# Three k tiles of the next projection's first output tile, multiplied ahead at each boundary, in a two-layer decoder trunk on one core

## What is computed

```python
for l in range(2):
    h = h + 0.5 * rmsnorm(swiglu(rmsnorm(h, g[FFN1_PRE]), w_in[l, 0], w_out[l, 0]), g[FFN1_POST])
    hn = rmsnorm(h, g[MIX_PRE])
    u_pool, q, k, v, gate_pool, gate_attn = split(hn @ w_in[l])
    y_pool = pool_mixer(u_pool)                 # causal means over 2, 4, 8, 16 tokens
    y_attn = swa_attention(q, k, v) @ w_attn_proj[l]
    merged = sigmoid(gate_pool) * y_pool + sigmoid(gate_attn) * y_attn
    h = h + rmsnorm(merged @ w_o[l], g[MIX_POST])
    h = h + 0.5 * rmsnorm(swiglu(rmsnorm(h, g[FFN2_PRE]), ...), g[FFN2_POST])
```

## Time and profile before

| | us |
|---|---|
| median of 3 runs (1190.07 to 1190.86) | 1190.37 |
| the profiled execution | 1191.37 |
| its span | 1189.3 |
| PE busy | 1179.4 (99%) |
| PEld busy | 1149.5 (97%) |
| DVE, ACT, POOL busy | 712.3, 541.1, 457.9 |

### The profile page before, as it was taken

One profiled execution on the slowest core, in us unless ns is written; L12 is line 12 of the kernel. 1 busy time (PEld: TensorE's weight loads), 2 busy tenths in 40 slices (PEclk: granted clock), 3 DMA queues, 4 the chain that ended last, 5 costly groups with the idle time before them and its releaser, 6 DMA issues.

```text
span 1189.3 us, 23831 instructions
## 1 busy us (share of the span) xinstructions
PE 1179.4 (99%) x9310; PEld 1149.5 (97%) x9310; DVE 712.3 (60%) x1050; ACT 541.1 (45%) x761; POOL 457.9 (39%) x521
## 2 busy tenths in 40 slices
PE   8999999999999999999999999999999999999997
PEld 7999999999999999999999999999999999999986
DVE  5755444868665865544477554447676658755542
ACT  6433334536553553333355333345466545544441
POOL 1855500207212476542128545112063124865600
PEclk9999999999999999999999999999999999999999
DMA  9754457373355355545636553573734653754540
GB/s 323 253 180 158 127 186 224 97 231 107 90 151 188 123 181 176 175 128 179 217 112 213 177 168 119 195 209 111 240 108 101 175 181 107 229 195 160 188 165 35
DMA packets 197997, 198.69 MB, mean 167 GB/s; under 512 B 4368, under 2 KB 190864, under 8 KB 197920
## 3 DMA queue, kind: packets, MB, share of 16 engines
q1 hardware_dynamic: 197600, 197.27, 52.4%
q10 hardware_dynamic: 320, 0.34, 0.1%
HBM read 196.54 MB, written 1.05 MB: 166 GB/s over the span
## 4 chain that ended last, share of the span: by engine, by line
PE 97%; DVE 2%; DMA 1%; SPq 0%; ACT 0%; issue 0%; DVEq 0%
PE bank L505 28%; PE bank L506 28%; PE bank L504 28%; PE bank L736 2%; PE bank L738 2%; PE bank L737 2%; PE bank L640 1%; PE bank L825 1%; PE bank L820 1%; PE bank L631 1%; PE bank L779 1%; PE bank L538 1%; DMA raw<-in_ffn_w_in 1%; PE bank L539 1%; PE bank L564 1%; PE bank L790 0%
## 5 line engine op out<-in xcount | busy, mean ns | idle before, releaser
L504 PE MATMUL bank<-x_hi,w_hi 128*128 128x272 f32 (+1 forms) x1988 | 572.1, 288 | 2.0 <-DVE w_lo L1607 1.4
L505 PE MATMUL bank<-x_lo,w_hi 128*128 128x272 f32 (+1 forms) x1988 | 570.5, 287 | 0.0
L506 PE MATMUL bank<-x_hi,w_lo 128*128 128x272 f32 (+1 forms) x1988 | 568.6, 286 | 0.0
L939 ACT ACTIVATE w_hi<-raw 128x2048 fp32r<-128x2048 f32 (+2 forms) x208 | 348.8, 1684 | 412.5 <-PE bank L506 398.3
L1240 DVE TENSOR_TENSOR w_lo<-raw,w_hi 128x2048 fp32r<-128x2048 f32 (+3 forms) x203 | 419.7, 2073 | 158.8 <-ACT w_hi L939 153.8
L504 PEld LDWEIGHTS bank<-x_hi,w_hi 128*128 128x128 f32 x1988 | 375.8, 189 | 4.0 <-DVE w_lo L1607 1.7
L505 PEld LDWEIGHTS bank<-x_lo,w_hi 128*128 128x128 f32 x1988 | 375.3, 189 | 0.3
L506 PEld LDWEIGHTS bank<-x_hi,w_lo 128*128 128x128 f32 x1988 | 373.7, 188 | 0.0
L1807 POOL TENSOR_TENSOR hid_hi<-silu,up_r 128x272 f32 x88 | 136.5, 1552 | 163.4 <-DVE up_r L1385 145.4
L505 PE MATMUL bank<-hid_lo,w_hi 128*128 128x272 f32 x528 | 152.3, 289 | 0.0
L506 PE MATMUL bank<-hid_hi,w_lo 128*128 128x272 f32 x528 | 151.9, 288 | 0.0
(11 more groups left out here) (205 smaller groups left out, 1276.4 us busy)
## 6 DMA issues: line engine op xcount, KB each, us to landing
raw<-in_ffn_w_in SPq DMA_DIRECT2D x86, 1024.0 KB, 5.1
raw<-in_w_in SPq DMA_DIRECT2D x24, 1024.0 KB, 5.7
raw<-in_ffn_w_out SPq DMA_DIRECT2D x24, 768.0 KB, 4.4
raw<-in_ffn_w_out SPq DMA_DIRECT2D x24, 640.0 KB, 4.0
raw<-in_ffn_w_out SPq DMA_DIRECT2D x10, 1024.0 KB, 5.0
raw<-in_w_in SPq DMA_DIRECT2D x16, 512.0 KB, 5.2
raw<-in_w_attn_proj SPq DMA_DIRECT2D x32, 256.0 KB, 4.6
raw<-in_w_o SPq DMA_DIRECT2D x8, 1024.0 KB, 5.7
```

Source lines behind the costliest of these rows:

```text
L504: pe.matmul(ps[:, t0:T], w[0], a_hi[:, t0:T], start=start, stop=False)
L505: pe.matmul(ps[:, t0:T], w[0], a_lo[:, t0:T], start=False, stop=False)
L506: return pe.matmul(ps[:, t0:T], w[1], a_hi[:, t0:T], start=False, stop=stop)
L939: last = act.activation(hi, w, ACT.Copy)
```

## The change

At each of the five boundaries, three k tiles (2, 3, 4 for n = 0 and 2; 1, 2, 3 for n = 1) of output tile 0 of the next projection are computed ahead and in two pieces. The new `h` of a tile is the old `h` plus a factor times `y` times the token's root; so the product with it is the product of old `h` (piece 0), plus the product of `y` with its gains (piece 1) times the root.

- PE: `keep_dense` and the bank opener go. Ahead of the spread it runs the 3 x 3 matmuls of piece 0, which go into the bank of output tile 0, behind it the 3 x 3 of piece 1, into a bank of their own. In `deep_three`, output tile 0 leaves out these three k tiles. The sum moves from ahead of tile 2 of k = 6 to ahead of tile 5, the spread from ahead of tile 2 of k = 7 to ahead of tile 4.
- ACT and DVE: 6 operands more each (`early_high`, `early_low`) before a boundary. They lie in idle slots of `x_hi` and `x_lo` (n = 0, 2) or of `o_hi` and `o_lo` (n = 1, once the attention projection has read them).
- ACT, in the pre-norm: it copies piece 1 out of its bank into `y` tile 0 behind `x_hi` tile 5, and makes the hi part of the next unit in four quarters, behind `x_hi` tiles 3, 4, 5 and 6, instead of behind the pre-norm.
- DVE: it multiplies piece 1 by the spread root (`scale_early`) behind `normed(7)`. It makes the lo part of the next unit ahead of var and no longer waits for POOL's power there. When it takes output tile 0, it adds piece 1 and then multiplies by `r` (`with_early`). At the start of a layer it makes the combined gains `g_out` with 3 small instructions.

```diff
+EARLY_K = ((2, 3, 4), (1, 2, 3), (2, 3, 4))
+EARLY_OLD, EARLY_OUT = 2, 5
...
+def early_before(n):
+    return n // 3 * 2 * sum(len(ks) for ks in EARLY_K) + 2 * sum(len(ks) for ks in EARLY_K[:n % 3])
...
-                        for c in range(6):
+                        for c in range(1 if k in EARLY_K[(q - 2) // 2 % 3] else 0, 6):
                             high(c, k, 0, T)
                     x_tile(x_at + k, l)
                     for c in range(6):
@@ -558,6 +578,8 @@
                             sum_part(q, l, 0)
                         if (k, c) == SPREAD_AT:
                             spread_rms(q, l)
+                        if c == 0 and k in EARLY_K[(q - 2) // 2 % 3]:
+                            continue
...
-            def keep_dense(n, by):
-
-                for _ in range(n):
-                    pe.matmul(warm[:, 0:SEQ], by[:, 0, META:META + P], by[:, 1, META:T], start=True, stop=True)
-
-            def open_banks(banks, by):
-
-                for b in banks[0:CUT_TILES]:
-                    pe.matmul(bank[b][:, 0:T], by[:, 0, META:META + P], zeros[:, 0:1].to_broadcast([P, T]), start=True, stop=False)
+            def early_products(n, l, u, which, b, t0):
+                ks = EARLY_K[n]
+                pe.wait_ge(early_lo, early_before(l * 3 + n) + (which + 1) * len(ks))
+                if which == 0:
+                    unit_split(u, l if n < 2 else l + 1)
+                    tile_free((T_FFN_OUT[0], T_WO, T_FFN_OUT[1])[n] + 6, l, 0)
+                for at, k in enumerate(ks):
+                    hi, lo = early_operand(n, which, at)
+                    last = products(bank[b], weights(u, k, 0), hi, lo, at == 0, which == 1 and at == len(ks) - 1, t0)
+                if which == 1:
+                    last.then_inc(early_done, 1)
...
-                    pe.transpose(bank[SPREAD_BANKS[q // 2]][:, first:first + n], rt[0:n, 0:1].to_broadcast([n, P]),
+                    pe.transpose(bank[SPREAD_BANK][:, 0:n], rt[0:n, 0:1].to_broadcast([n, P]),
...
-                keep_dense(WARM_RMS, hid_hi)
+                n, u, (b, b_out) = 2 * f, (U_K, U_FFN_IN[0])[f], EARLY_BANKS[2 * f]
+                early_products(n, l, u, 0, b, 0)
                 spread_rms(4 * f + 1, l)
-                keep_dense(WARM_X, hid_hi)
-                open_banks((KVQ_BANKS, FFN_BANKS)[f], hid_hi)
+                early_products(n, l, u, 1, b_out, 0)
...
+            def early_high(n, l, which, at, columns):
+                k = EARLY_K[n][at]
+                src = (h, y)[which]
+                act.activation(early_operand(n, which, at)[0], src[:, k, :], ACT.Copy, scale=columns[:, k:k + 1]
+                               ).then_inc(early_hi, 1)
+            def pre_norm(n, columns, h_before, u, u_layer):
+                parts = split_parts(u, len(NEXT_SPLIT_AT))
                 square(n, 0, h[:, 0, :], h_ready, h_before + 1)
                 for k in range(1, KD):
+                    if k == EARLY_OLD:
+                        act.wait_ge(early_done, n // 2)
                     x_high(columns, h_before, k)
+                    if k == EARLY_OUT:
+                        act.activation(y[:, 0, :], bank[EARLY_BANKS[n // 2 % 3 - 1][1]][:, 0:T], ACT.Copy).then_inc(early_taken, 1)
+                    if k in NEXT_SPLIT_AT:
+                        if k == NEXT_SPLIT_AT[0]:
+                            act.wait_ge(raw_landed[u % RING], landed_at(u, u_layer))
+                            act.wait_ge(unit_done, u_layer * UNITS + u + 1)
+                        w, hi, _ = parts[NEXT_SPLIT_AT.index(k)]
+                        last = act.activation(hi, w, ACT.Copy)
+                        if k == NEXT_SPLIT_AT[-1]:
+                            last.then_inc(hi_done, 1)
                     if k > 1:
                         square(n, k - 1, h[:, k - 1, :], h_ready, h_before + k)
                 square(n, KD - 1, h[:, KD - 1, :], h_ready, h_before + KD)
...
-                if l + f > 0:
-                    split_hi(u0 + 3, l)
...
+                act.wait_ge(layer_consts, l + 1)
+                n, g_x = 2 * f, (g_cur[:, 2 * KD:3 * KD], g_next)[f]
+                for at in range(len(EARLY_K[n])):
+                    early_high(n, l, 0, at, g_x)
+                for at in range(len(EARLY_K[n])):
+                    early_high(n, l, 1, at, g_out[:, n * KD:(n + 1) * KD])
...
+                act.wait_ge(unit_done, l * UNITS + U_WO + RING)
+                for at in range(len(EARLY_K[1])):
+                    early_high(1, l, 0, at, g_cur[:, 4 * KD:5 * KD])
...
+                    if m == EARLY_K[1][-1]:
+                        for at in range(len(EARLY_K[1])):
+                            early_high(1, l, 1, at, g_out[:, KD:2 * KD])
...
+                for n, by in enumerate((0.5, 1.0, 0.5)):
+                    g_y, g_x = (g_all[:, ds(l * (NORMS * KD) + (2 * n + i) * KD, KD)] for i in (1, 2))
+                    dve.scalar_tensor_tensor(out=g_out[:, n * KD:(n + 1) * KD], in0=g_y, scalar=by, in1=g_x,
+                                             op0=ALU.mult, op1=ALU.mult)
...
+            def early_low(n, l, which, at, columns):
+                k = EARLY_K[n][at]
+                src = (h, y)[which]
+                hi, lo = early_operand(n, which, at)
+                dve.wait_ge(early_hi, early_before(l * 3 + n) + which * len(EARLY_K[n]) + at + 1)
+                dve.scalar_tensor_tensor(out=lo, in0=src[:, k, :], scalar=columns[:, k:k + 1], in1=hi.bitcast(F32),
+                                         op0=ALU.mult, op1=ALU.subtract).then_inc(early_lo, 1)
+            def early_lows(n, l, which, columns):
+                for at in range(len(EARLY_K[n])):
+                    early_low(n, l, which, at, columns)
+            def with_early(n, l, b, out, scale):
+                dve.wait_ge(early_scaled, l * 3 + n + 1)
+                dve.tensor_tensor(y[:, 0, :], bank[b][:, 0:T], y[:, 0, :], ALU.add).then_inc(early_sum, 1)
+                dve.wait_ge(early_sum, l * 3 + n + 1)
+                return dve.tensor_tensor(out, y[:, 0, :], scale[:, :], ALU.mult)
...
+                def scale_early():
+                    t0 = blocks(2 * n + 1, l)[0][0]
+                    dve.wait_ge(early_taken, l * 3 + n + 1)
+                    dve.tensor_tensor(y[:, 0, t0:T], y[:, 0, t0:T], spread[:, t0:T], ALU.mult
+                                      ).then_inc(early_scaled, 1)
...
+                    if k + 1 == KD - 1:
+                        scale_early()
...
+                    if j == 0 and early is not None:
+                        n, early_l = early
+                        with_early(n, early_l, FFN_BANKS[0], gate_r[:, 0, :], r).then_inc(tile_read, 1)
+                        continue
...
+                    split_lo(u0 + 3, l)
                     mean_square(4 * f, l)
-                    dve.wait_ge(rt_ready, l * NORMS + 4 * f + 1)
-                    split_lo(u0 + 3, l)
                     take_rms(4 * f, l)
-                    take_gate(f, l, 0)
+                    take_gate(f, l, 0, early=(1, l) if f == 1 else (2, l - 1))
...
+                n = 2 * f
+                early_lows(n, l, 0, (g_cur[:, 2 * KD:3 * KD], g_next)[f])
+                early_lows(n, l, 1, g_out[:, n * KD:(n + 1) * KD])
...
+                split_lo(41, l)
                 mean_square(2, l)
-                dve.wait_ge(rt_ready, l * NORMS + 3)
-                split_lo(41, l)
                 take_rms(2, l)
-                take(U_K, F_KV, l, KVQ_BANKS[0:2], lambda j, ps: dve.tensor_tensor(kT[:, j, :], ps, r[:, :], ALU.mult))
+                take(U_K, F_KV, l, KVQ_BANKS[0:2], lambda j, ps: with_early(0, l, KVQ_BANKS[0], kT[:, 0, :], r) if j == 0
+                     else dve.tensor_tensor(kT[:, j, :], ps, r[:, :], ALU.mult))
...
+                early_lows(1, l, 0, g_cur[:, 4 * KD:5 * KD])
                 take_y(0)
                 take_y(1)
+                early_lows(1, l, 1, g_out[:, KD:2 * KD])
...
-WARM_RMS, WARM_X = 10, 7
 CUT_TILES = 1
-SPREAD_BANKS = (0, 2, 2)
+EARLY_BANKS, SPREAD_BANK = ((6, 0), (0, 2), (0, 2)), 1
 META_STEP = 6
 HIGH_FIRST = 2
-SUM_AT, SPREAD_AT = (6, 2), (7, 2)
+SUM_AT, SPREAD_AT = (6, 5), (7, 4)
+NEXT_SPLIT_AT = (3, 4, 5, 6)
 FFN_BANKS, KVQ_BANKS = (0, 1, 6, 3, 4, 5), (6, 1, 2, 3, 4, 5)
```

40 lines of the change are left out of this document (27 added, 13 removed).

## The result

The changed kernel takes **1194.25 us** (median of 7 executions, 1192.18 to 1196.17) against 1190.07 us for the kernel before on the same chip (7 executions, 1189.84 to 1190.91): ratio 1.0035, 95% interval 1.0025 to 1.0045. It is 4.2 us slower. The forecast was 1189.3 with a range up to 1192.0: wrong in its sign, and outside the range. The profiled execution took 1195.46 us, its span 1193.6.

What follows compares the result with a forecast made beforehand. PE bounds the kernel, busy 99% of the span. Savings by layer: n = 0, 1.06 and 0.9; n = 1, -0.1 and -1.5; n = 2, 0.8; 1.1 us less in all gives 1189.3 us, range 1186.2 to 1192.0.

Steps and rivals of the forecast that it cites:

- part 5: End of the pre-norm: stepping both queues has POOL's sixth sum asked for at 224.36, the seventh standing behind DVE's split.
- part 4: ACT in the pre-norm: quarters and piece 1's copy make it as busy as DVE; squares come 0.3 to 0.5 late.
- part 2: DVE's pace in k = 1 to 4: of 1.12 us, all stays for n = 0 and 2, 0.75 or 0.45 for n = 1.
- The clock: PE's clock after the mixer: a few tenths of idle time should not lower it; no chance set aside.
- Part 1: PE's stream: 9 matmuls per boundary leave deep_three, 1.12 us each, 5.6 over five; the spread starts no later.
- Part 3: Operands made ahead after the mixer: post_var 0.87 us late in layer 1, 0.05 in layer 0; nothing before n = 0 and 2.
- Part 5, n = 1: Pre-norm's sum: one split of 2.29 us holds up the seventh sum; PE waits 0.8 (layer 0) and 1.1 (layer 1).
- The reading in which both share the speed: DVE and POOL ports: both go on slowed, the seventh sum takes 1.5 to 2 us and costs nothing; 1187.4 us.
- n = 0: Pre-norm's sum: it slips between two half splits; PE waits 0.05 us in layer 0, 0.2 in layer 1.
- n = 2: Spread at the new layer: var stands behind columns and split, at 228.7; PE waits 0.3 to 0.4 us.
- Behind the projection: After the projection: DVE is earlier, its split done; with_early costs one instruction of 0.44 us and nobody waits.
- The rival "slower": End of k = 6: split always ahead of seventh sum, sixth behind last x_lo; 2.6 more, 1193.0 us; chance 0.11.

Runs made afterwards that it cites:

- E5: Changed kernel with scale_early moved behind update 7 and ACT's copy of piece 1 behind the square of tile 4: 1191.68 us, ratio 1.0008 to the kernel before.
- E8: The changed kernel itself, timed once more beside the other runs: 1194.36 us, ratio 1.0032 to the kernel before.
- E7: Changed kernel with the next unit's split behind the pre-norm, sum and spread at old places, scale_early and piece 1's copy moved later: 1188.87 us, ratio 0.9984.
- E3: Kernel before with only the order moves (ACT's quarters, lo part ahead of var, later sum and spread), no products ahead: 1190.92 us, ratio 0.9999.
- E2: Changed kernel with only DVE's lo part of the next unit put back behind var and POOL's power: 1192.65 us, ratio 1.0012.
- E4: Changed kernel with the next unit's split back behind the pre-norm on both ACT (one whole hi part) and DVE: 1192.25 us, ratio 1.0010.
- E10: Kernel before without its unread matmuls between the norm's sum and the spread and behind it (10 and 7 per boundary): 1197.63 us, ratio 1.0057.
- E11: E7 with the combined gains made in FFN 1's output stage and nothing made ahead at layer 1's mixer boundary: 1187.51 us, ratio 0.9974.
- E1: Changed kernel with unread matmuls put back where PE waits, ahead of late sums and spreads: 1193.61 us, ratio 1.0021 to the kernel before.
- E12: E11 with eight unread matmuls ahead of PE's wait for first_lo in the first projection: 1187.51 us, ratio 0.9976.

## Why the prediction was wrong

**The step that failed** is the stepping of the two queues in part 5: "the sixth sum is asked for at 224.36". On that clock it came at 225.34 less 0.34 for the later start, 225.00: 0.64 us late. I had counted `scale_early` as 0.36 to 0.44 us of DVE and the copy of piece 1 as a shift of ACT, but had not followed rightly what they push: update 7 into the fifth sum (0.86 instead of 0.44), x_hi 7 behind it, and the squares queued behind x_hi 7. E5 shows it by moving the two: the sixth sum comes 0.73 us earlier, and the time falls by 2.7 us (medians); in the table the five boundaries give 2.3 of it, with n = 1 of layer 0 held against E8, where the clock didn't fall either. The blame I gave to ACT's quarters in part 4 ("the squares come 0.3 to 0.5 late") is right in size (0.3, E5 against E7), was in the stepping already (224.36 is 16.08 us after the norm's first sum; E3 and E5, with the quarters, have 16.00 and 15.99), and cost nothing where the split is behind (E2 against E4).

**A second term was mis-sized: what the saved matmuls bring.** In E5 PE's waits are the forecast's almost to the tenth (0.69 and 1.10 at the sums of n = 1, 0.41 at n = 2, 0.74 for the late root, none at n = 0). Yet its five boundaries take together 0.1 us more than before, where the forecast had 1.15 less. So 1.25 us more were lost. By estimate 0.8 of it is the refilling of the pipeline behind these four waits, 0.2 each, which the forecast left out; the rest is that the 1.12 per boundary don't stay whole (part 2 below).

**The clock.** "The few tenths of idle time ... should not lower it ... No chance is set aside for it." It fell in both profiled executions of the changed kernel, at different waits, for 1.55 us in one. In E10 it fell at five boundaries of five, at 1.1 to 2.4 us each. The Trainium skill ("TensorE: Matmul & The Clock Gate", Part 1) has the idle array at half its clock. The trace agrees on the two levels, and it goes further: in E10 PE stood still for no more than 1.18 us at a time, with matmuls in between, and the clock fell. My ground for setting it aside, that the first slices show a full clock though PE is not always busy there, was no ground: the nines of the page can't show a fall of 3.4 us, and in E3 and E11 the clock did fall there; in the execution of before it happened not to. And the unread matmuls were worth 7.0 us to the kernel before (E10).

Point by point:

- *Part 1, 9 matmuls or 1.12 us per boundary*: they are gone (45 in all). The spread of layer 0, n = 0 starts 2.47 us after the norm's first sum, before 2.52: right.
- *Part 2, "all of the 1.12 stays" for n = 0 and 2*: 0.80 and 0.83 at best (E7). In E7's trace at n = 0 of layer 0 the first real product starts 4.09 us after the norm's first sum instead of 3.94, and PE stands at the pre-norm's sum just as the seventh sum ends (17.66 and 17.61 us after the norm's first sum; before, 18.61 and 17.59). Before, there was 1.0 us of room between the two, less than the 1.12 to be saved. The later place of the sum, which the forecast reckoned with, gives room back; what it would keep without other waits, no run shows.
- *Part 3, the late root after the mixer*: post_var 0.87 late forecast; it starts at 994.17, 3.18 after the earlier trace rows, of which 2.40 are the whole kernel's shift: 0.78. Right in size and place, though the working has it twice: a split that ends at 992.0 would make post_var 1.0 late, not 0.87. In layer 0 the spread comes 0.05 later, as said.
- *Part 5, n = 1*: waits of 0.8 and 1.1 forecast, 1.17 and 1.57 idle measured, 0.2 more each with the refilling. The rule that the ports are locked for a whole instruction held: at n = 1 the split, asked for 0.06 us after the sixth sum, first stands behind it (2.87 us instead of 2.29), and then the seventh sum stands behind the split: the pair takes 3.54 us instead of some 1.9. The Trainium skill says so in "SBUF — State Buffer", section "Who interferes with whom", and the trace agrees. The reading in which both share the speed (1187.4) is refuted: it gave the seventh sum 1.5 to 2 us, and it took 2.62.
- *n = 0*: 0.05 and 0.2 forecast, 0.48 and 0.64 idle measured, by the late sixth sum.
- *n = 2*: 0.3 to 0.4 at the spread, 0.89 measured: var stands behind columns and split, as said, and all of it was 0.65 later (var at 626.75, 229.35 on the clock of the first boundary, against 228.7).
- *Behind the projection*: "nobody waits there" was right for the changed kernel. But E4 shows what the split's place ahead of var was good for: without it, with PE 1.1 us earlier, each boundary waits 0.45 to 0.72 us idle for that split. I had named this cover nowhere.
- *The rival "slower"* came nearest, with a chance of 0.11. Its deciding point was 228.4 on that clock; at n = 1 of layer 0 the seventh sum ended at 420.09, which is 228.7. Its prices fit too (0.3 kept at n = 0 of layer 0, where the table has 0.32; 0 at n = 2, 0.01), and its 1193.0 lacks mainly the clock. But the way there was another, and so the fit is in part luck: the sixth sum did not wait behind the last x_lo (it took 0.77), it was asked for late, and at n = 2 the seventh sum stood behind no split.

In sum, for the profiled executions, the forecast had 1.1 us less and the measurement 4.3 more, 5.4 us apart: 2.3 for the late sixth sum, 1.55 for the clock, 1.25 for the refilling and the savings that don't stay whole, 0.3 at the start. By itself the late sum, the step that failed, does not explain the sign: with it put right and no fall of the clock (E5) the kernel is level with the one before. How much of the median is the clock's, only the mean granted clock tells: by the estimate in E1, 0.7 to 1.1 falls per execution.

## What to carry to other kernels

When work leaves the engine that bounds a kernel, every hand-over behind it must come earlier by the same amount; look first how much room each of them has. Follow every small instruction that you put ahead of such a hand-over through all queues, up to the instruction that this engine waits for, before calling it 0.4 us. Price a wait of TensorE as its idle time plus the refilling (0.2 to 0.3 us here), and plus a possible stretch at half clock. Unread matmuls in a wait are no waste: whoever removes them must show that the idle time is gone too.

## What the runs showed of the hardware

- Short idle stretches in a dense program can halve TensorE's clock: with 1.0 to 1.2 us and then 0.6 to 0.7 us of waiting at one boundary always (E10, five of five), behind a single wait of 0.7 to 1.9 us sometimes (after: behind 1.17, not behind 1.57; E8: behind 0.74, not behind 1.16). The stretch at 0.5 starts between the last 0.3 us of a wait (E10, n = 1 of layer 0) and 2.2 us behind it, and takes 3.4 us; at n = 1 of layer 0 of E10 it takes 6.8, which is the dearest of the five.
- The clock also fell in the first 20 us of some executions, where PE waits 0.5 to 1.9 us for a lo part: in E3 (1.75 us) and E11 (1.86 us), not in the other profiled ones (up to 1.67 us). These two have the latest "first" of the table (210.72 and 210.20, the others up to 209.53), so it is a part of the spread between executions. That filling this wait narrows the spread (E12) is not shown.
- A TensorE wait shown as 0.52 us of idle time cost 0.8 (E4).
- Two instructions of DVE and POOL that block each other run one after the other, but for 0.14 to 0.20 us: x_lo ends 0.29 us behind POOL's sum instead of 0.49, update 7 ends 0.30 behind it instead of 0.44, and the seventh sum 0.61 behind the split instead of 0.77 (after, n = 1).
- The kernel before took 1190.07, 1190.95, 1190.95, 1190.65 and 1190.27 us (medians) on five occasions: a difference of 0.5 us between two kernels needs common runs.
